# Dilated attention: two score units move into the value projections, and the group weights into the tail of the scores stage

## The reference, cut to the dilated attention

```python
for g, (window, dilation) in enumerate(DIL_GROUPS):
    o, lse = strided_window_attention(qkv[:, :, 0, g], qkv[:, :, 1, g], qkv[:, :, 2, g],
                                      dilation, window // dilation,
                                      rel_bias[:, g * Hg:(g + 1) * Hg])
    outs.append(o)
    lses.append(lse)
outs = jnp.stack(outs)
wts = jax.nn.softmax(jnp.stack(lses), axis=0)
o = jnp.einsum('gbshd,gbsh->bshd', outs, wts.astype(outs.dtype)).reshape(B, S, Hg * dh)
return o @ w_o
```

## Time and profile before

| what | us |
|---|---|
| median of 3 runs | 2165.7 (2162.51 to 2168.86) |
| the profiled execution | 2166.3 |
| its span in the trace | 2164.6 |
| PE busy | 2046.9 (95%) |
| DVE busy | 1153.2 (53%) |
| ACT busy | 860.7 (40%) |
| POOL busy | 344.4 (16%) |

### The profile page before, as it was taken

How to read it: one execution, slowest core, us unless ns; L and a number is a source line. 1 busy time by engine, 2 the same in 40 slices (tenths; PEclk the granted TensorE clock), 3 DMA queues, 4 the chain that set the end, 5 groups by cost and what they waited for, 6 DMA issues and landing times. The chain is left out here.

```text
span 2164.6 us, 28154 instructions
## 1 busy us (share of the span) xinstructions
PE 2046.9 (95%) x11502; PEld 1614.6 (75%) x11502; DVE 1153.2 (53%) x1452; ACT 860.7 (40%) x1242; POOL 344.4 (16%) x310
## 2 busy tenths in 40 slices
PE   8999889899988989998999999999998989999998
PEld 5777877567787768744778888877888877888886
DVE  4445647544564753244468547635332856745763
ACT  4245424524542451355344324333122735422432
POOL 1200616020061620134220000022000012000002
PEclk9999999999999999999999999999999989999999
DMA  5211102221110222200223232234221012223221
GB/s 225 77 59 39 41 20 99 97 79 59 40 41 23 95 78 97 99 29 1 78 80 109 81 111 98 77 102 143 92 91 51 1 59 78 92 94 111 94 89 66
DMA packets 30564, 167.48 MB, mean 77 GB/s; under 512 B 2827, under 2 KB 9411, under 8 KB 14692
## 3 DMA queue, kind: packets, MB, share of 16 engines
q1 hardware_dynamic: 30004, 164.90, 22.1%
q10 hardware_dynamic: 432, 0.79, 0.1%
HBM read 159.35 MB, written 10.00 MB: 78 GB/s over the span
## 5 line engine op out<-in xcount | busy, mean ns | idle before, releaser
L301 PE MATMUL psum<-inputs_high,weights_high 128*128 128x512 f32 x928 | 383.2, 413 | 20.9 <-DVE inputs_low L249 12.8
L302 PE MATMUL psum<-inputs_low,weights_high 128*128 128x512 f32 x928 | 367.6, 396 | 0.0
L303 PE MATMUL psum<-inputs_high,weights_low 128*128 128x512 f32 x928 | 367.2, 396 | 0.0
L2072 PE MATMUL psum<-inputs_high,weights_high 128*128 128x512 f32 x704 | 276.4, 393 | 3.9 <-DVE weights_low L2064 3.4
L2073 PE MATMUL psum<-inputs_low,weights_high 128*128 128x512 f32 x704 | 274.0, 389 | 0.0
L2074 PE MATMUL psum<-inputs_high,weights_low 128*128 128x512 f32 x704 | 274.0, 389 | 0.0
L254 DVE TENSOR_TENSOR weights_low<-weights_raw,weights_high 128x2048 fp32r<-128x2048 f32 x68 | 159.8, 2351 | 177.6 <-ACT weights_high L243 177.6
L301 PEld LDWEIGHTS psum<-inputs_high,weights_high 128*128 128x128 f32 x928 | 176.4, 190 | 78.6 <-DVE inputs_low L249 17.0
L302 PEld LDWEIGHTS psum<-inputs_low,weights_high 128*128 128x128 f32 x928 | 176.5, 190 | 41.1 <-issue 4.8
L303 PEld LDWEIGHTS psum<-inputs_high,weights_low 128*128 128x128 f32 x928 | 176.2, 190 | 40.3
L243 ACT CAST weights_high<-weights_raw 128x2048 fp32r<-128x2048 f32 x68 | 129.1, 1898 | 194.0 <-PE psum L303 178.2
(11 more groups left out here) (371 smaller groups left out, 3269.1 us busy)
## 6 DMA issues: line engine op xcount, KB each, us to landing
weights_raw<-w_stream SPq DMA_DIRECT2D x116, 1024.0 KB, 4.8
weights_raw<-w_down SPq DMA_DIRECT2D x32, 704.0 KB, 3.9
residual_parked<-residual SPq DMA_DIRECT2D x2, 2048.0 KB, 10.0
residual_back<-residual_parked SPq DMA_DIRECT2D x2, 2048.0 KB, 7.7
residual<-x_t SPq DMA_DIRECT2D x2, 1024.0 KB, 9.1
bias_by_row<-bias_rows SPq DMA_DIRECT2D x2, 1024.0 KB
bias_by_row<-bias_rows SPq DMA_DIRECT2D x1, 1536.0 KB
out_t<-residual SPq DMA_DIRECT2D x5, 256.0 KB, 2.3
```

What stands on the lines that cost most here:

```text
L301: pe.matmul(out, hi, self.ahi[:, k], start=start and b == 0, stop=False)
L302: pe.matmul(out, hi, self.alo[:, k], start=False, stop=False)
L303: mm = pe.matmul(out, lo, self.ahi[:, k], start=False, stop=stop and b == blocks - 1)
L2072: pe.matmul(out, wh, hi, start=start, stop=False)
```

## The change

Units 0 and 1 of the scores stage get their scores, biases, maxima and exponentials in the projections, while the values of the last group are made: scores(0) ahead of chunk u=0 and scores(1) ahead of chunk u=1 of g=2, into PSUM banks 6 and 7. The two units have their buffers in tiles 0 to 3 of `num`; the later units keep the two buffers of the scores stage, and the waits that they made on units 0 and 1 are gone from PE's queue. PE begins the scores stage with turn(0). The group weights are made at the end of the scores stage: the small matmuls behind turn(13), DVE's steps behind turned(14), the exponential on ACT between the copies of the last two tiles. Their tiles lie in `k.norm` then.

```diff
+EARLY_UNITS = 2
+def unit_scores(pe, out, q, kk, unit):
+    g, t, h0, heads, keys = unit
+    for hd in range(h0, h0 + heads):
+        rows = slice(64 * (hd % 2), 64 * (hd % 2) + 64)
+        at = (hd - h0) // 2 * keys * P
+        f = 4 * g + hd // 2
+        mm = pe.matmul(out[:, hd % 2, at:at + keys * P], q[rows, f, t * P:(t + 1) * P],
+                       kk[rows, f, (t + 1 - keys) * P:(t + 1) * P], start=True, stop=True)
+    return mm
+def unit_exp(act, scores, top, total, unit, hd):
+    g, t, h0, heads, keys = unit
+    at = hd % 2 * T + (hd - h0) // 2 * keys * P
+    x = scores[:, at:at + keys * P]
+    return act.activation(x, x, ACT.Exp, bias=top[:, TT * g + t, hd:hd + 1], accum_out=total[:, TT * g + t, hd:hd + 1])
...
@@ dilated_projections, tensor @@
                         st.split(pe, s, first_v + 2 * g + u)
+                        if g == DIL_GROUPS - 1:
+                            pe.wait_ge(s.freed, n_features)
+                            pe.wait_ge(s.column, 2)
+                            if u >= 1:
+                                pe.wait_ge(s.biased, u)
+                            unit_scores(pe, ps[:, 6:8], q, kk, units[u]).then_inc(s.scores, 1)
@@ dilated_projections, scalar @@
                     st.high(act, s, first_v + 2 * g + 1, 1)
+                    if g == DIL_GROUPS - 1:
+                        for n, unit in enumerate(units):
+                            act.wait_ge(s.biased, n + 1)
+                            for hd in range(unit[2], unit[2] + unit[3]):
+                                unit_exp(act, sc[:, n], top, total, unit, hd).then_inc(s.exp, 1)
@@ dilated_projections, vector @@
                 for c in range(first_v + 1, DIL_CHUNKS):
                     st.low(dve, s, c, c % 2)
+                dve.wait_ge(s.table, 16 * DIL_GROUPS)
+                for n, unit in enumerate(units):
+                    dst, tab = unit_biases(tables, sc[:, n], unit)
+                    g, t, h0, heads, keys = unit
+                    dve.wait_ge(s.scores, n + 1)
+                    for y in range(2):
+                        dve.tensor_tensor(dst[:, y], ps[:, 6 + y].rearrange("p (h w) -> p h w", h=heads // 2), tab[:, y],
+                                          ALU.add).then_inc(s.half, 1)
+                    dve.wait_ge(s.half, 2 * n + 2)
+                    dve.tensor_reduce(top[:, TT * g + t, h0:h0 + heads].rearrange("p (h y) -> p y h", y=2), dst, AX_X,
+                                      ALU.max, negate=True).then_inc(s.biased, 1)
...
@@ dilated_scores, tensor @@
-                    if n >= 2:
-                        pe.wait_ge(s.biased, n - 1)
+                    if n >= 2 + EARLY_UNITS:
+                        pe.wait_ge(s.biased, n - 1 - EARLY_UNITS)
...
-                    pe.wait_ge(s.exp, exps(n + 1))
+                    if n >= EARLY_UNITS:
+                        pe.wait_ge(s.exp, exps(n + 1))
...
-                scores(0)
-                scores(1)
                 for n in range(n_units + 1):
                     if n < n_units:
                         turn(n)
                     if n + 2 < n_units:
                         scores(n + 2)
+                    if n == n_units - 2:
+                        for c in range(4):
+                            for t in range(TT):
+                                mm = pe.matmul(ps[32 * t:32 * t + 32, class_bank, c * 16:c * 16 + 16], by_class(ident, 4)[:, c],
+                                               stats[:, t].rearrange("p y h -> p (y h)"), start=True, stop=True)
+                        mm.then_inc(s.classed, 1)
                     if n >= 1:
                         values(n - 1)
@@ dilated_scores, vector @@
-                bias(0)
-                bias(1)
                 for n in range(n_units):
                     turned(n)
                     if n + 2 < n_units:
                         bias(n + 2)
+                dve.wait_ge(s.classed, 1)
+                step(dve.tensor_copy(first.rearrange("p t y h -> p (t y h)"), ps[:, class_bank, 0:TT * 2 * DIL_HEADS]))
...
+                step(dve.tensor_tensor(e[:, 1:], rest[:, :, :, 0], over_groups(low, 2), ALU.subtract))
+                dve.wait_ge(s.exp, exps(n_units))
+                dve.wait_ge(s.group_exp, 1)
...
+                step(dve.tensor_tensor(e, e, over_groups(den, DIL_GROUPS), ALU.mult))
@@ dilated_scores, scalar @@
-                for n in range(n_units + 3):
+                for n in range(EARLY_UNITS, n_units + 3):
                     if n < n_units:
-                        exps(n)
+                        exp_of(n)
+                    if n - 3 == n_units - 1:
+                        act.wait_ge(s.step, 5)
+                        act.activation(e, e, ACT.Exp, scale=-1.0).then_inc(s.group_exp, 1)
                     if n - 3 in tiles:
                         copy_out(n - 3)
```

More of the change, by code:

```diff
@@ L2455, in _, with group_weights, part, dilated_scores @@
                         .then_inc(s.added, 1)
-def dilated_scores(nc, k, q, kk, v, tables, num, top, total):
+def group_weights(k):
+    flat = k.norm[:].rearrange("p a t -> p (a t)")
+    n = TT * DIL_HEADS
+    def part(at, groups):
+        return flat[:, at * n:(at + groups) * n].rearrange("p (g t h) -> p g t h", g=groups, t=TT)
+    return named(first=flat[:, 0:2 * n].rearrange("p (t y h) -> p t y h", t=TT, y=2), low=part(2, 1)[:, 0], den=part(3, 1)[:, 0],
+                 e=part(4, DIL_GROUPS), prod=part(4 + DIL_GROUPS, DIL_GROUPS), w0=part(4 + 2 * DIL_GROUPS, 1)[:, 0])
+def dilated_scores(nc, k, q, kk, v, tables, num, stats, early, top, total):
     ps, con = k.ps, k.con
     ident = con[:, K_IDENT:K_IDENT + P]
-    units = [(0, 0, 0, 8, 1)] + [(0, t, h0, 4, 2) for t in range(1, TT) for h0 in (0, 4)] \
-        + [(g, t, 0, 8, 1) for g in (1, 2) for t in range(TT)]
+    units = dilated_units()
     n_units = len(units)
     tiles = [n for n, (g, t, h0, heads, _) in enumerate(units) if h0 + heads == DIL_HEADS]
-    with ExitStack() as stack, phase(nc, "scores", "half", "biased", "exp", "turned", "turned_read", "out", "out_copy") as s:
-        sc = stack.enter_context(sbuf(nc, "scores", [P, 2, 2 * T], F32))
+    with ExitStack() as stack, phase(
+            nc, "scores", "half", "biased", "exp", "turned", "turned_read", "out", "out_copy", "classed", "step", "group_exp") as s:
+        w = group_weights(k)
+        first, low, den, e, prod = w.first, w.low, w.den, w.e, w.prod
+        rest = stats[:, TT:].rearrange("p (g t) y h -> p g t y h", g=2)
+        class_bank = 2 * ((n_units - 2) % 2)
+        def over_groups(v, groups):
+            return v.unsqueeze(1).to_broadcast([P, groups, TT, DIL_HEADS])
+        late = stack.enter_context(sbuf(nc, "scores", [P, 2, 2 * T], F32))
         pt = stack.enter_context(sbuf(nc, "weights_turned", [P, 2, 8, P], F32))
+        def scores_of(n):
+            return (early if n < EARLY_UNITS else late)[:, n % 2]
         def exps(n):
-            return sum(u[3] for u in units[:n])
+            return sum(u[3] for u in units[EARLY_UNITS:n])
         def tile_of(n):
@@ L2483, in scores @@
                 def scores(n):
-                    g, t, h0, heads, keys = units[n]
                     b = 2 * (n % 2)
-                    if n >= 2:
-                        pe.wait_ge(s.biased, n - 1)
[L2488 to L2494, removed]
+                    if n >= 2 + EARLY_UNITS:
+                        pe.wait_ge(s.biased, n - 1 - EARLY_UNITS)
+                    unit_scores(pe, ps[:, b:b + 2], q, kk, units[n]).then_inc(s.scores, 1)
                 def turn(n):
-                    pe.wait_ge(s.exp, exps(n + 1))
+                    if n >= EARLY_UNITS:
+                        pe.wait_ge(s.exp, exps(n + 1))
                     if n >= 1:
@@ L2620, in _ @@
             def _(pe):
-                for c in range(rate):
-                    for t in range(TT):
-                        mm = pe.matmul(ps[32 * t:32 * t + 32, 4, c * 16:c * 16 + 16], by_class(ident, rate)[:, c],
-                                       stats[:, t].rearrange("p y h -> p (y h)"), start=True, stop=True)
-                mm.then_inc(s.classed, 1)
-                pe.wait_ge(s.weight, 1)
                 for t in range(TT):
```

103 lines of the change are left out of this document (46 added, 57 removed).

## The result

| | before | after |
|---|---|---|
| median of 7 runs | 2166.58 us (2162.51 to 2168.86) | 2155.3 us (2149.8 to 2157.3) |
| the profiled execution | 2166.3 us | 2155.93 us |
| its span in the trace | 2164.6 us | 2154.2 us |
| mean granted clock | 0.979 | 0.984 |

The ratio is 0.9944, with a 95% interval of 0.9934 to 0.9954: by it the change is 12.1 us faster, with bounds at 10.0 and 14.3, and the two medians are 11.3 us apart. The forecast was 11.3 us, to 2154.5 us, from the 2165.7 us of the first three runs.

A forecast was written before the change was run, and what follows sets the result against it. PE was taken as the bound, busy 95% of the span. Gains of 6.5 us (scores stage's begin net of projections), 3.8 (tail) and 1.0 (clock) sum to 11.3 us, forecasting 2154.5 us; range 2152.5 to 2157 us, chance 0.60.

The forecast's parts named there:

- part 4: Clock at the tail, in spread and merge: less time at the lower level gives 1.0 us.
- part 2: Projections: PE pays 2.2 us for the 24 early score matmuls, bounds 2.0 and 4.1; the rest stays covered.
- Part 1: Begin of the scores stage: turn(2) 7.0 us behind the first PE instruction instead of 15.74, giving 8.7 us.
- Part 3: Tail of the scores stage: PE reaches the spread matmuls at 1731.4 in place of 1735.17, giving 3.8 us.
- (a): Rival: the scores stage begins at the lower clock, losing 3.5 us; 2159.8 us with costlier breaks; chance 0.11.
- (c): Rival: clock stays down in the scores stage, 3.0 us more per unit; slower; chance 0.04, shared with unseen waits.
- (b): Rival: DVE's chain holds the block open, tail gives only 0.7 us, 2157.5 us; chance 0.12 with other tail shortfalls.
- (d): Rival: clock at the tail goes well, half or all of 6.1 us won, 2150 to 2152 us; chance 0.13.

The follow-up runs named there:

- front_only: Only the two early units in the projections, with the group weights left in the output stage as in the kernel before: 2160.81 us, ratio 0.9967 to before.
- tail_only: Only the group weights moved to the scores stage's tail, no early units, against the kernel before: 2161.33 us, ratio 0.9977.
- together: The changed kernel with both early units' scores made at one place, ahead of chunk u=1 of g=2: 2155.24 us.
- best: The changed kernel with `small_spread` and `together` joined, and the group weights' exponential ahead of the last but one tile's copy: 2152.16 us, ratio 0.9929 to before.
- after_again: The changed kernel run once more, unaltered, in a later series on another chip: 2153.44 us, ratio 0.9931 to before.
- extra_scores: The changed kernel with unit 0's scores made six surplus times in g=1, with no wait at those places: 2163.68 us, ratio 0.9985 to before.
- small_spread: The changed kernel with the 16 spread matmuls made into 4, using a mask and one more DVE step: 2151.2 us, ratio 0.9926 to before.
- spread_later: The changed kernel with the 16 spread matmuls behind the fourth merged tile instead of ahead of the first: 2156.5 us, ratio 0.9949 to before.

## Why the prediction was right, point by point

The mechanism was as forecast, but for half of part 4: each of its parts is found in the traces, and `front_only` and `tail_only` show the two halves alone. The sizes of parts 2 and 4 were off, and in opposite directions: part 2 cost 0.6 us more than forecast and part 4 gave 0.4 more, so that the sum comes closer (11.0 us for 11.3) than its terms do.

**Part 1.** Turn(2) was forecast 7.0 us behind the stage's first instruction and came at 6.89 (1673.37 less 1666.48). The wait ahead of it was foreseen, with 0.6 us, and is 0.74. From there to turn(14) both kernels take 47.72 us, so the steady pace is unchanged, as forecast. The stage's begin gives 8.85 us: 7.02 from scores and idle time that are gone, and 1.8 because turn(0) and scores(2), which took 3.90 us at the lower level of the clock, now take 2.06.

**Part 2** is the term that was sized wrong. PE pays 2.81 us (26.36 less 23.55 us from the last evacuation of g=1 to the scores stage's first matmul), where I took 2.2. I had allowed 0.1 us for a break; by `together` one is worth 0.46 us. The bound of 4.1 us held. The cover was as described: bias(0) ended at 1647.4, 5 us ahead of the place where PE asks for it, and ACT's delay was gone by the last tile but two. Parts 1 and 2 gave 6.0 us, for 6.5; `front_only` shows them alone.

**Part 3.** 3.8 us forecast, 3.6 measured, 3.6 in `tail_only` too. The missing 0.15 us is the block's end. From turn(14) to the next block's first PE instruction it took 5.54 us before (and in `front_only`) and 5.89 after, 0.35 us more where I had 0.2, because PE now begins 0.55 us behind DVE's last step, and had begun 0.30 us behind ACT's last copy. The exponential did wait for the copy of the last but one tile, by 0.2 us as `best` shows, and the small matmuls cost nothing: PE still has 0.27 us of idle ahead of turn(14), of the 1.07 it had.

**Part 4.** 1.0 us forecast, 1.4 measured in the profiled execution. The fall did come, and the lower level lasted for 3.0 us less from the spread's start on. 1.6 us of these are the rise that came earlier against the spread's start (8.2 us behind it, 9.8 before), which I had reckoned with. The other 1.3 are the fall, which came 1.3 us behind the spread's start where it had come 3.9 us ahead of it, and which I had not. What the clock costs comes out of the traces. In the seven that have the old spread ahead of the merge, spread to product is 13.9 to 14.1 us plus half of the time that the stretch was at the lower level (9.8 us of it before, 6.8 in the changed kernel, 3.4 in `after_again`). But the term has no single value: in the eight traces with the new tail the clock is at the lower level for 3.4, 6.8 or, in `extra_scores`, 10.2 us, and the changed kernel alone shows the first two. Held against the same 18.78 us of before, `after_again` gives 3.0 us for this term, and `extra_scores`, with the same instructions there, gives nothing. So it is luck that the profiled execution came within 0.4 us of the forecast. The bounds, from 0.7 us lost to 6.1 won, held it, but the upper one was set too high. At the full level the merge takes 10.8 us, not 9.6: that is before's 13.52 less half of the 5.4 us at the lower level, and 12.61 less half of 3.4 in `tail_only` gives 10.9. All that a clock at the full level could have won was 4.9 us.

**The rivals.** (a), the cold begin, fell: the clock is at 1.00 in the slices from 1666 on, with no fall at the boundary. (c) fell with it. By the busy times by stretch, the granted clock of the whole scores stage is 1.00 where it was 0.95:

```profile
1666.00:1726.50 60.50, 58.05 (x560) 51.94 (x560) 53.14 (x80) 42.12 (x182) 0.00 (x0) 1.00 0.01 2
```

This stage now opens with transposes. By the rule of the Trainium skill that was weighed (TensorE: Matmul & The Clock Gate, Part 4 on the PE-mode transpose), its begin should have been slow; the trace shows no such thing, and the measurement decides. It shows only this mixture: the transposes alternate with score matmuls, and the values had ended only 1 us before. How a row of transposes alone would fare no run shows. (b), a tail that holds the block open, is there to the size of the 0.35 us of part 3: DVE's chain, not the last copy, sets the end. Its extra step in `small_spread` comes back in full (0.3 us), and so does the 0.2 us that it is shortened by in `best`. (d), a good clock at the tail, is what `after_again` and `tail_only` had, with 3.0 us won.

## What to carry to other kernels

A stage whose first result needs a chain over several engines can have that chain run under the stage before it, where those engines are idle; the gain is what leaves the stage's head less what the same work costs at its new place. Here that was 4.99 us of idle, 2.03 of scores and 1.8 of a lower clock behind the idle time, less the 2.81 paid in the projections: 6.0 us. Put such inserted matmuls in one place, because each switch of the stream costs by itself (0.46 us here). At a stage's end, see which engine's last instruction opens the next block, and count each step on it in full. And where the clock falls near such a boundary, as it did in every trace here, work made there is dear: moving the spread matmuls behind four tiles of the merge won nothing, and making them from a quarter of the instructions won 1.1 us in the trace.

## What the runs showed of the hardware

A switch from matmuls of 128 rows and 512 columns to those of 64 rows, and back, costs PE 0.46 us, of which 0.23 is seen in the first matmul after it (0.63 us in place of 0.40, with its follower 0.46 us behind in place of 0.23).

The 16 spread matmuls of 32 rows and 8 columns are 32 records in the trace. They took 2.44 and 2.47 us at the full level of the clock (`tail_only`, `spread_later`) and 4.48 to 4.51 us at the lower one (`extra_scores`, before and `front_only`): 0.08 and 0.14 us a record. At the full level they didn't keep the clock there: it fell 0.2 us behind their end in `tail_only` and in `spread_later`, and 0.3 us before it in `after_again`. In `spread_later` PE had been busy for 8 us by then.

The next block's first PE instruction came 0.55 us behind the last instruction of the block when that was DVE's (changed kernel, `tail_only`, `small_spread`, `best`), and 0.30 us when it was ACT's (before).

At the tail the lower level lasted 13.7 us before, 10.2 us in `front_only` and in `extra_scores`, 6.8 us in the changed kernel and in `best`, and 3.4 us in `tail_only`, `after_again`, `together` and `small_spread`; in `spread_later` it lasted 3.4 us twice. `extra_scores`, the changed kernel and `after_again` have the same instructions at this place, and had it for 10.2, 6.8 and 3.4 us; what decides between these the runs don't show.
